# Modulation steps moved out of the attention loops and set in pairs, and earlier splits between convolution taps

## What is computed

```
mod = silu(c) @ w_mod[l] + b_mod[l];  modc = silu(c_ctx) @ w_mod[l] + b_mod[l]
sh1, sc1, gt1, sh2, sc2, gt2 = split(mod, 6)                # six sections of 1024
h = rms_norm(x, g_pre_mix) * (1 + sc1) + sh1
y = token_mixer(h, hc, ...)     # conv of 31 taps, pool, differential attention, gated merge
x = x + gt1 * rms_norm(y, g_post_mix)
h = rms_norm(x, g_pre_ffn) * (1 + sc2) + sh2
x = x + gt2 * rms_norm(swiglu(h, w_ffn_in, w_ffn_out), g_post_ffn)
```

## Time and profile before

| | us |
|---|---|
| median of 3 runs | 2370.2 (2367.84 to 2386.32) |
| the profiled execution | 2384.31 |
| its span in the trace | 2382.1 |
| PE busy in the span | 2243.6 (94%) |
| DVE busy | 1344.9 (56%) |
| ACT busy | 893.0 (37%) |
| mean granted TensorE clock | 0.966 |

### The profile page before, as it was taken

How to read it: one execution, slowest core, us unless ns; L and a number is a source line. 1 busy time by engine, 2 the same in 40 slices (tenths; PEclk the granted TensorE clock), 3 DMA queues, 4 the chain that set the end, 5 groups by cost and what they waited for, 6 DMA issues and landing times. The chain is left out here.

```text
span 2382.1 us, 33171 instructions
## 1 busy us (share of the span) xinstructions
PE 2243.6 (94%) x13304; PEld 1877.4 (79%) x13304; DVE 1344.9 (56%) x2015; ACT 893.0 (37%) x1400; POOL 191.5 (8%) x244
## 2 busy tenths in 40 slices
PE   4999998999999999999999898999899999998998
PEld 2767745877887777788785897998788898897996
DVE  2467666465453333237956666664584565565664
ACT  2322155323252222225226545444343443444443
POOL 2082100010010000003410000000100000000000
PEclk8999999999999999999999998999896999999999
DMA  7444325333325554234422454665641666452663
GB/s 256 133 133 133 102 89 155 94 89 92 109 75 142 142 142 133 89 115 124 120 84 76 141 162 140 184 189 192 146 130 36 178 191 189 142 160 77 189 195 123
DMA packets 428659, 320.82 MB, mean 135 GB/s; under 512 B 25810, under 2 KB 379724, under 8 KB 428508
## 3 DMA queue, kind: packets, MB, share of 16 engines
q1 hardware_dynamic: 426108, 310.77, 44.0%
q0 software_dynamic: 2368, 7.93, 1.1%
q10 hardware_dynamic: 32, 0.01, 0.0%
HBM read 317.62 MB, written 1.05 MB: 134 GB/s over the span
## 5 line engine op out<-in xcount | busy, mean ns | idle before, releaser
L295 DVE TENSOR_TENSOR split<-raw,split 128x1024 fp32r<-128x1024 f32 x500 | 595.6, 1197 | 622.7 <-ACT split L292 621.6
L306 PE MATMUL PS<-HH,split 128*128 128x256 f32 (+1 forms) x2552 | 829.8, 325 | 43.5 <-DVE split L295 22.3
L307 PE MATMUL PS<-HL,split 128*128 128x256 f32 (+1 forms) x2552 | 812.8, 318 | 0.0
L308 PE MATMUL PS<-HH,split 128*128 128x256 f32 (+1 forms) x2552 | 812.1, 318 | 0.0
L292 ACT ACTIVATE split<-raw 128x1024 fp32r<-128x1024 f32 x500 | 506.4, 1026 | 464.3 <-PE PS L308 368.2
L306 PEld LDWEIGHTS PS<-HH,split 128*128 128x128 f32 x2552 | 489.6, 192 | 101.9 <-DVE split L295 28.5
L308 PEld LDWEIGHTS PS<-HH,split 128*128 128x128 f32 x2552 | 488.9, 192 | 36.1
L307 PEld LDWEIGHTS PS<-HL,split 128*128 128x128 f32 x2552 | 489.7, 192 | 34.6 <-issue 0.5
L306 PE MATMUL PS<-split,UH 128*128 128x512 f32 x416 | 167.4, 402 | 0.0
L308 PE MATMUL PS<-split,UL 128*128 128x512 f32 x416 | 164.9, 396 | 0.0
L307 PE MATMUL PS<-split,UH 128*128 128x512 f32 x416 | 164.9, 396 | 0.0
(11 more groups left out here) (267 smaller groups left out, 2569.8 us busy)
## 6 DMA issues: line engine op xcount, KB each, us to landing
raw<-in_w_in_dram SPq DMA_DIRECT2D x120, 512.0 KB, 4.3
raw<-in_w_ffn_in_dram SPq DMA_DIRECT2D x88, 512.0 KB, 4.7
raw<-in_l_w_gate_up_dram SPq DMA_DIRECT2D x88, 512.0 KB, 3.9
G<-in_w_mod_dram SPq DMA_DIRECT2D x86, 512.0 KB, 4.0
raw<-in_w_ffn_out_dram SPq DMA_DIRECT2D x44, 512.0 KB, 3.5
raw<-in_l_w_down_dram SPq DMA_DIRECT2D x44, 512.0 KB, 4.6
raw<-in_l_w_in_dram SPq DMA_DIRECT2D x30, 512.0 KB, 4.6
raw<-in_w_attn_out_dram SPq DMA_DIRECT2D x16, 512.0 KB, 3.7
```

Of the source, the lines that this page charges most:

```text
L295: eng.tensor_tensor(c["low"], c["raw"], c["high"].bitcast(F32), ALU.subtract).then_inc(low_done, 1)
L306: pe.matmul(out, a[0], b[0], start=first, stop=False)
L307: pe.matmul(out, a[0], b[1], start=False, stop=False)
L308: return pe.matmul(out, a[1], b[0], start=False, stop=last)
```

## The change

The steps keep their number, 96, and their arithmetic; 32 steps leave the attention loops. L0's branch phase gets 16 steps in 8 pairs, L0's FFN now has 40 steps in 20 pairs instead of 24 single ones, and L0's projections do their 24 steps in 12 pairs, one in three points. A pair issues its two loads together, before its eight matmuls. The turns at blocks 14, 22 and 30 of L0's attention and at block 14 of L1's go to the branch phase (one) and to the FFN (three). Between the convolution's taps in L0 DVE asks with other keys: in taps 0 to 6 with the pool tiles' instead of the last GLU tile's, and after tap 22 with v's first half instead of the last turned k tile.

```diff
@@ -766,45 +766,47 @@
 
     SHIFT_1, SCALE_1, GATE_1, SHIFT_2, SCALE_2, GATE_2 = range(6)
     groups = [(l, s) for l in range(DEPTH) for s in range(6)]
-    phases = {"start": groups[0:2], "L0_proj": groups[2:5], "L0_attn": groups[5:8], "L0_ffn": groups[8:11], "L1_attn": groups[11:12]}
-    turn_points = {"start": {11: groups[0]}, "L0_proj": {13: groups[2], 25: groups[3]}, "L0_attn": {2: groups[4], 14: groups[5], 22: groups[6], 30: groups[7]},
-                   "L0_ffn": {17: groups[8], 31: groups[9], 43: groups[10]}, "L1_attn": {14: groups[11]}}
-
-    def mod_step(phase, point):
+    phases = {"start": groups[0:2], "L0_proj": groups[2:5], "L0_branch": groups[5:7], "L0_ffn": groups[7:12]}
+    pairs_at = {"L0_proj": range(0, 36, 3), "L0_branch": (0, 2, 5, 8, 11, 13, 16, 19), "L0_ffn": range(3, 43, 2)}
+    turn_points = {"start": {11: groups[0]}, "L0_proj": {13: groups[2], 25: groups[3]}, "L0_attn": {2: groups[4]}, "L0_branch": {12: groups[5]},
+                   "L0_ffn": {5: groups[6], 13: groups[7], 21: groups[8], 29: groups[9], 37: groups[10], 43: groups[11]}}
+
+    def mod_steps(phase, point):
 
         if phase not in phases:
-            return None
-        if phase == "L0_proj":
-            q = 2 * (point // 3) + point % 3 if point % 3 < 2 else None
-        elif phase == "L0_ffn":
-            point = point - 3
-            q = 3 * (point // 5) + (0, 1, None, 2, None)[point % 5] if point % 5 in (0, 1, 3) else None
+            return []
+        if phase == "start":
+            qs = [point]
+        elif point in pairs_at[phase]:
+            at = pairs_at[phase].index(point)
+            qs = [2 * at, 2 * at + 1]
         else:
-            q = point if phase == "start" else point - 4
-        return q if q is not None and 0 <= q < KT * len(phases[phase]) else None
+            qs = []
+        return [q for q in qs if q < KT * len(phases[phase])]
 
     def mod_pe(T, pe, phase, point):
 
         if phase in turn_points and point in turn_points[phase]:
-            mod_turn(T, pe, turn_points[phase][point], SPARE_BANK if phase.endswith("attn") else None)
-        q = mod_step(phase, point)
-        if q is None:
-            return
-        l, sec = group = phases[phase][q // KT]
-        k = q % KT
-        i, w = T.load(rows(A["w_mod"][l], k, 1, sec * D, D), (1, D), split=False,
-                      ring="raw" if phase == "start" and q % (RAW[0] + MOD_RING) < RAW[0] else "mod",
-                      home_free={"L0_ffn": (S("L0_y_added"), 4), "L1_attn": (S("L0_ffn_added"), 4)}.get(phase))
-        if k == 0:
-            T.open(("mod",) + group)
-        for j in range(4):
-            ins = pe.matmul(bank(("mod",) + group)[QUAD * j:QUAD * (j + 1), 0:SEQ], silu_c[:, 2 * k:2 * k + QUAD],
-                            w[:, 0, SEQ * j:SEQ * (j + 1)], start=(k == 0), stop=(k == KT - 1))
-        if k < KT - 1:
-            T.mark(ins)
-        else:
-            T.close(ins, ("mod",) + group)
-        T.used(i)
+            mod_turn(T, pe, turn_points[phase][point])
+        steps = mod_steps(phase, point)
+        loaded = []
+        for q in steps:
+            l, sec = phases[phase][q // KT]
+            loaded.append(T.load(rows(A["w_mod"][l], q % KT, 1, sec * D, D), (1, D), split=False,
+                                 ring="raw" if phase == "start" and q % (RAW[0] + MOD_RING) < RAW[0] else "mod",
+                                 home_free={"L0_ffn": (S("L0_y_added"), 4)}.get(phase)))
+        for q, (i, w) in zip(steps, loaded):
+            group, k = phases[phase][q // KT], q % KT
+            if k == 0:
+                T.open(("mod",) + group)
+            for j in range(4):
+                ins = pe.matmul(bank(("mod",) + group)[QUAD * j:QUAD * (j + 1), 0:SEQ], silu_c[:, 2 * k:2 * k + QUAD],
+                                w[:, 0, SEQ * j:SEQ * (j + 1)], start=(k == 0), stop=(k == KT - 1))
+            if k < KT - 1:
+                T.mark(ins)
+            else:
+                T.close(ins, ("mod",) + group)
+            T.used(i)
 
     def mod_turn(T, pe, group, among=None):
 
@@ -817,10 +819,10 @@
 
     def mod_act(act, phase, point):
 
-        q = mod_step(phase, point)
-        if q is None or q % KT != KT - 1:
+        last = [q for q in mod_steps(phase, point) if q % KT == KT - 1]
+        if not last:
             return
-        group = phases[phase][q // KT]
+        group = phases[phase][last[0] // KT]
         g = groups.index(group)
         wait_result(act, ("mod",) + group)
         if g >= 2:
@@ -1197,18 +1199,23 @@
                     else:
                         T.close(ins, (L + "o", o))
                         milestones[(L + "head", i - 3)] = milestones[(L + "o", o)]
-                mod_pe(T, pe, L + "attn", i)
+                if i in turn_points.get(L + "attn", {}):
+                    mod_turn(T, pe, turn_points[L + "attn"][i], SPARE_BANK)
 
             def branch(name, number, gate_col, w, kts, pair, ready):
                 for j in range(KT):
                     i, ws = T.load(rows(w_in, 0, KT, COL_G + gate_col * D + j * P, P), (KT, P))
                     tile_t(T, pe, (name + "_gate", j), ws, KT, 0, own, n)
                     T.used(i)
+                    if number < 2:
+                        mod_pe(T, pe, L + "branch", 2 * KT * number + 2 * j)
                     if j == 0:
                         ready()
                     iy, wy = T.load(rows(w, 0, kts, j * P, P), (kts, P))
                     tile_t(T, pe, (name, j), wy, kts, 0, both(pair, n), n)
                     T.used(iy)
+                    if number < 2:
+                        mod_pe(T, pe, L + "branch", 2 * KT * number + 2 * j + 1)
                     if number == 1:
                         gate_pe(T, pe, l, 0, j - 2)
 
@@ -1330,7 +1337,6 @@
                     if i >= 4:
                         wait_result(act, (L + "head", i - 4))
                     read_out(act.activation(AT[:, i % 2, 0:w], bank(key)[:, 0:w], ACT.Copy), key)
-                mod_act(act, L + "attn", i)
                 if i == len(us) - 1:
                     split_until(act, (L + "pt", i - 2))
             now["hold"] = False
@@ -1353,6 +1359,9 @@
                         wait_read(act, (L + ("yc", "ya", "yb")[(done - 2) // KT], (done - 2) % KT))
                     c = ROW_GATE + 8 * gc + j
                     read_out(act.activation(SG[:, done % 2, 0:n], bank(key)[:, 0:n], ACT.Sigmoid, bias=cols[:, l, 0, c:c + 1]), key)
+                    if nm != "yb":
+                        for k in range(2):
+                            mod_act(act, L + "branch", 2 * done + k)
                     done += 1
                     if nm == "yc" and j == NCH:
                         for k in range(NCH):
@@ -1525,13 +1534,19 @@
                         ins.then_inc(S(L + "conv"), 1)
                 if tap < 7:
 
-                    split_until(dve, (L + "glu", NCH - 1), AHEAD + 1 + tap)
+                    if l:
+                        split_until(dve, (L + "glu", NCH - 1), AHEAD + 1 + tap)
+                    else:
+                        split_until(dve, (L + "pool", min(tap // 2, 3)))
                 elif tap - 7 < len(ROPES):
                     rope_sin(*ROPES[tap - 7])
                     mod_dve(dve, L + "proj", 12 + tap - 7)
                 else:
 
-                    split_until(dve, (L + "k_rot", 7), min(tap - 20, 5))
+                    if l:
+                        split_until(dve, (L + "k_rot", 7), min(tap - 20, 5))
+                    else:
+                        split_until(dve, (L + "v", 0, 3), min(tap - 22, 4))
 
             key = (L + "mean",)
             wait_result(dve, key)
@@ -1640,6 +1655,9 @@
                         dve_link(dve, dve.tensor_tensor(MT[:, j, 0:n], MT[:, j, 0:n], GY[:, done % 2, 0:n], ALU.add))
                     if nm == "yb":
                         split_value(dve, MTH[:, j, 0:n], MTL[:, j, 0:n], MT[:, j, 0:n]).then_inc(S(L + "merged"), 1)
+                    if nm != "yb":
+                        for k in range(2):
+                            mod_dve(dve, L + "branch", 2 * done + k)
                     done += 1
                     if others:
                         others.pop(0)()
```

## The result

The changed kernel took 2393.48 us (median of 8 runs, 2388.25 to 2396.79), the kernel before in the same rounds 2378.26 (8 runs, 2367.84 to 2391.63): a ratio of 1.0066 with a 95% interval of 1.0033 to 1.0098. The forecast was 2356.2, the range 2341 to 2374. The change costs 15.2 between the medians, where a gain of 14 was forecast; the measured time lies 37.3 over the forecast one.

A forecast was written before the change was run, and what follows sets the result against it. PE, busy 94%, was taken as the bound: steps cost full price where PE never waits, less in the attention's three-engine chain. Terms summed to -14.0 off the 2370.2 us median: 2356.2 us, range 2341 to 2374.

The forecast's parts named there:

- Price of a step and of a pair: Where PE hardly waits, a single step costs 0.67 us and a pair 1.10; FFN sum +6.8 with three turns.
- Part 1, first wait: L0's first taps: earlier splits remove PE's 4.86 us wait and its half-clock stretch, nothing late behind; gain 7.1 us.
- Part 1, second wait: End of L0's convolution: chunks split between taps remove the 3.26 us wait and slow product behind it; gain 5.9 us.
- part 2: L0's projections: 12 pairs cost 13.2 us instead of 15.8 for 22 single steps and one pair; gain 2.6 us.
- Part 3: L0's projections, point 4: chunk late behind two step loads, 3.2 us wait and half clock; loss 4.2 us (0.5 to 4.5).
- Parts 4 and 5: Attention without steps: L0 gains 15.3 us (13 to 17), wide blocks 2.99 and narrow 1.92 each; L1 gains 3.4.
- the rival that it would fall there: With PE idling in every attention block the clock falls: 2365.4 us, or 2389.6 with wide blocks too; chance 0.10.
- Part 6: L0's branch phase: 8 pairs, a turn and a 1.1 us wait behind DVE's reciprocal; loss 9.3 us (8 to 14).
- pairs hold back the weights: Rival: every pair in FFN and branch phase ends in a 1.7 us wait, +48, 2404 us; chance 0.08.
- the wide half of the clock rival: Half clock in L0's 12 wide attention blocks too, 5.0 against 2.99 us each: +24 more, 2389.6 us.

The follow-up runs named there:

- e8: Kernel before with both new split keys and POOL's pooling held until seven taps are done, steps as before: 2372.14 us, ratio 0.9962.
- e6: Kernel before with only its PSUM bank rotation moved on by four when L1 begins: 2387.93 us, ratio 1.0034.
- e2: Kernel before with only the key after tap 22 changed, v's first half for the last turned k tile: ratio 0.9986.
- e12: Changed kernel with nine transposes on PE behind the second model's first scores, their result overwritten: 2368.35 us, ratio 0.9962.
- e10: Changed kernel, banks as they are, with PE waiting before the second model's first scores for ACT's read of V: 2371.42 us.
- e1: Kernel before with only the key in taps 0 to 6 changed to the pool tiles': ratio 1.0009.
- e3: Changed kernel with both old split keys, so the moved and paired steps alone: 2399.72 us, ratio 1.0109.
- e11: Changed kernel, POOL held for seven taps, banks put back, pairs at projection points 1, 4, ... 34, branch 0, 3, ... 21, nine transposes: 2345.22 us, ratio 0.9871.

## Why the prediction was wrong, step by step

The 37.3 us between forecast and result have two parts. One is the fall of the clock in the second model's attention: the forecast started from the faster group (2370.2), the changed kernel shows the slower one alone (2387.7 before), 17.5. The other is the stages, slower group against slower group: 2393.5 - 2387.7 = +5.8 where -14.0 was forecast, 19.8. Two steps of the sum make most of that: the first taps (10.9 off) and the branch phase (7.7 off).

- **Price of a step and of a pair:** right. In the FFN 20 pairs for 24 single steps cost 6.2 where 6.8 was forecast.
- **Part 1, first wait:** wrong, and the largest error among the terms. The step that failed is "18.64 / 7 = 2.66 a tap": the taps were so fast because POOL stood still behind 28 instructions in a row. With splits between them a tap takes 5.2 to 5.8, the split for point 13 is done at 144.1 and not near 130, and -7.1 became +3.8. The sentence "nothing is late behind it" was built on DVE, ACT and loads; POOL's timeline, where an instruction of 19.75 us stood beside neighbours of 1.1, wasn't read. With POOL held back the term measures -7.1 (e8).
- **Part 1, second wait, and part 2:** right, -8.0 for -8.5.
- **Part 3:** right in size (+4.7 for +4.2), and partly by luck. PE first waited 1.93 for the pair's own second load, which the forecast didn't have, and then 2.69 for the chunk. But e8 and e6, with single steps, show +4.6 and +3.3 there as well (waits of 3.70 and 3.50), and the kernel before and e2 1.5: this wait varies from execution to execution, and no run shows how much of it the pair adds. With the first pair at point 1 or 2 both waits are gone in all three traces (-3.1).
- **Parts 4 and 5:** right. L0's attention -14.3 for -15.3; ten wide blocks now take (352.63 - 322.32) / 10 = 3.03 each, nine narrow ones 17.57 / 9 = 1.95, for 2.99 and 1.92. The clock stayed full, so the rival that it would fall there was wrong, though PE waits in every block. L1 -3.1 for -3.4.
- **Part 6:** the mechanism was right, the size not: +17.0 for +9.3, outside its bounds of 8 to 14. The pairs with short waits cost about what was reckoned (+10.2 in e12, where no wait of 0.9 or more stands there). The rest hangs on how late the loads behind a pair land. The chunk of the second wait landed 9.8 us after the pair's first load ahead of it was issued in the changed kernel; in e12, where PE waits 0.47 there, 8.2. In six traces of the same order +10.2, 10.9, 12.3, 12.6, 13.7 and 17.0 were seen, so the profiled execution is the worst of them, and five lie inside the bounds. Three points apart gives +8.6. So the rival "pairs hold back the weights" was right in the branch phase and wrong in the FFN, where two points are 11.4 us.
- **Small slips:** 110.6 + 1.2 + 2 x 2.66 is 117.1, not 117.2, and the wide half of the clock rival adds up to 2389.4, not 2389.6; nothing hangs on either.
- **Not in the forecast at all:** the banks. It asked what the moved instructions cost, not what state they share with the rest. The turns' banks shifted everything behind them, and with it the half clock came, judged by the times, in 33 of 38 executions of the kernels with shifted banks and neither e10's wait nor the transposes (e6's 2377 counted with it), against 38 of 95 before. This is the larger part of the measured difference of 15.2: without the more frequent fall 5.8 are left, and e12, which has all of the change but not the fall, is level with the faster half of the kernel before (2368.3 and 2368.2). It is not a gain either: what the attention gave, the taps and the branch phase took.

What stays open: what lets POOL in. In the kernel before its instruction took 19.75 us for 1.1, kept out also by the three splits behind the taps; in e1 it came in behind the first split after it asked, in the changed kernel and e3 after the tap that was running. That splits between taps open the way is shown, the rule isn't. Open is also why one execution of the same kernel has the fall and the next has not, and why a wait of 0.57 us more makes it rarer; shown is that it takes the gap of 1.47. How late the loads behind a pair land wasn't set by any run either.

## What to carry to other kernels

Before an instruction stream is cut or moved, look at every engine in that stretch for an instruction that is far longer than its neighbours of the same shape (here 19.75 us beside 1.1): something may be keeping it out, and the change may let it in. Ask of a moved instruction which counters it advances (banks, ring slots, parity), and look at the waits of stages far behind it. And if the times of a kernel lie in two groups, find the stage that separates them before costing anything: here nine throwaway transposes in a gap of 1.5 us were worth some 20 us in an execution that had the fall, more than the whole gain forecast.

## What the runs showed of the hardware

- DVE's taps and POOL's additions took turns: DVE's tap instruction went from 0.74 to 1.23 us in the median, up to 1.78, and its split from 1.22 to 2.10. In the kernel before POOL got no turn: its instruction, begun at 115.01 amid DVE's 28, took 19.75 us.
- An idle time of TensorE of 1.47 us between short groups was followed, in seven of twelve traces, by 41 to 61 us at 1.2 GHz; where it was 44 us the same attention took 55.3 and not 35.5 us. With 0.34 us idle in its place this came in none of 18 executions (e11, e12; two traces and the times).
- A wait of 0.5 us ahead of that gap made the kernel faster in the median, from 2393 to 2371 (e10), by making the fall rarer: 4 of 12 executions, where it was 8 of 8.
